# Two layout turns of a two-block network on one Trainium2 core: TensorE transposes replaced by VectorE block transposes and SBUF transfers

## What is computed

```python
h = rmsnorm(x, norm1_g);  proj = h @ w_in
uv, s5_in, qkv, gates = ...                      # columns of proj
y_a = u * (tril(W_s) @ rmsnorm(v) + b_s)         # u, v = halves of gelu(uv), per chunk of 128 tokens
y_b = s5_mixer(s5_in)                            # linear state space scan, gelu, a gate g @ w_glu
y_c = stick_breaking_attention(q, k, v)
merged = sum(sigmoid(gates) * (y_n @ w_branch[n]))
x = x + merged @ w_out;  x = x + relu(rmsnorm(x) @ w_mlp_in)**2 @ w_mlp_out;  x = rmsnorm(x)
```

## Time and profile before

| | |
|---|---|
| three timed runs | 2872.83 us median, 2872.74 to 2873.57 |
| the profiled execution | 2873.68 us, of which its span is 2872.0 |
| TensorE matmuls busy | 2855.1 us, 99% of the span |
| weight loads, VectorE, ScalarE busy | 2358.0, 1813.5, 1368.5 us |
| granted TensorE clock | 1.0 |
| DMA | 588.38 MB, 205 GB/s |

### The profile page before, as it was taken

One profiled execution on the slowest core, in us unless ns is written; L12 is line 12 of the kernel. 1 busy time (PEld: TensorE's weight loads), 2 busy tenths in 40 slices (PEclk: granted clock), 3 DMA queues, 4 the chain that ended last, 5 costly groups with the idle time before them and its releaser, 6 DMA issues.

```text
span 2872.0 us, 33479 instructions
## 1 busy us (share of the span) xinstructions
PE 2855.1 (99%) x13486; PEld 2358.0 (82%) x13486; DVE 1813.5 (63%) x1939; ACT 1368.5 (48%) x1534; POOL 2.0 (0%) x7
## 2 busy tenths in 40 slices
PE   9999999999999999999999999999999999999998
PEld 7888878888888888888888888888888888888887
DVE  7688854466765556555567678866675555556555
ACT  6644444564455444444446444454455444444444
POOL 0000000000000000000000000000000000000000
PEclk9999999999999999999999999999999999999999
DMA  9566656546867666665667656656667666666664
GB/s 317 153 201 198 205 163 196 169 156 199 256 220 216 211 203 214 203 209 194 202 218 225 208 182 198 201 195 204 204 216 234 221 204 193 212 202 215 203 209 165
DMA packets 347354, 588.38 MB, mean 205 GB/s; under 512 B 21056, under 2 KB 81088, under 8 KB 346560
## 3 DMA queue, kind: packets, MB, share of 16 engines
q1 hardware_dynamic: 346768, 585.93, 64.1%
q10 hardware_dynamic: 432, 0.32, 0.0%
HBM read 556.81 MB, written 2.10 MB: 195 GB/s over the span
## 4 chain that ended last, share of the span: by engine, by line
PE 95%; DVE 3%; ACT 1%; issue 1%; DMA 0%; SPq 0%; DVEq 0%; ACTq 0%
PE ACC L633 93%; DVE WL L1308 1%; PE TB L579 0%; ACT WH L883 0%; DMA RAW<-in_w_in_dram 0%; PE TB L693 0%; DVE HT L1707 0%; DVE CA L1829 0%; DVE WGC L1877 0%; PE TB L726 0%; PE TB L729 0%; PE TB L735 0%; DVE ZCb L1682 0%; PE TB L781 0%; PE TB L835 0%
## 5 line engine op out<-in xcount | busy, mean ns | idle before, releaser
L1308 DVE TENSOR_TENSOR WL<-RAW,WH 128x1024 fp32r<-128x1024 f32 (+1 forms) x1023 | 1229.9, 1217 | 832.9 <-ACT WH L883 828.7
L883 ACT ACTIVATE WH<-RAW 128x1024 fp32r<-128x1024 f32 (+1 forms) x1023 | 1064.2, 1054 | 1120.0 <-PE ACC L633 797.2
L633 PE MATMUL ACC<-WH,XTH 128*128 128x512 f32 (+1 forms) x1692 | 662.1, 391 | 5.0 <-DVE WL L1308 3.4
L633 PE MATMUL ACC<-WH,XTL 128*128 128x512 f32 (+1 forms) x1692 | 655.6, 387 | 0.0
L633 PE MATMUL ACC<-WL,XTH 128*128 128x512 f32 (+1 forms) x1692 | 655.3, 387 | 0.0
L633 PE MATMUL ACC<-WH,XBL 128*128 128x512 f32 x1024 | 398.4, 389 | 0.0
L633 PE MATMUL ACC<-WH,XBH 128*128 128x512 f32 x1024 | 398.4, 389 | 0.0
L633 PE MATMUL ACC<-WL,XBH 128*128 128x512 f32 x1024 | 398.3, 389 | 0.0
L633 PEld LDWEIGHTS ACC<-WH,XTH 128*128 128x128 f32 x1692 | 317.8, 188 | 74.1 <-DVE WL L1308 6.7
L633 PEld LDWEIGHTS ACC<-WH,XTL 128*128 128x128 f32 x1692 | 317.7, 188 | 65.7
L633 PEld LDWEIGHTS ACC<-WL,XTH 128*128 128x128 f32 x1692 | 318.0, 188 | 62.7
(11 more groups left out here) (274 smaller groups left out, 1611.9 us busy)
## 6 DMA issues: line engine op xcount, KB each, us to landing
RAW<-in_w_in_dram SPq DMA_DIRECT2D x255, 512.0 KB, 4.3
RAW<-in_w_mlp_in_dram SPq DMA_DIRECT2D x128, 512.0 KB, 4.2
RAW<-in_w_mlp_out_dram SPq DMA_DIRECT2D x128, 512.0 KB, 4.9
RAW<-in_w_up_dram SPq DMA_DIRECT2D x128, 512.0 KB, 4.1
RAW<-in_w_down_dram SPq DMA_DIRECT2D x128, 512.0 KB, 4.8
RAW<-in_w_gate_dram SPq DMA_DIRECT2D x96, 512.0 KB, 4.3
YT<-HT SPq DMA_DIRECT2D x208, 128.0 KB, 2.7
RAW<-in_w_branch_dram SPq DMA_DIRECT2D x48, 512.0 KB, 4.3
```

What stands on the lines that cost most here:

```text
L633: ins = e.matmul(ACC[:, 2 * (b % 2) + half, 0:n], p[:, k, xs], q[:, t, 0:n], start=(k == 0 and m == 0), stop=(k == nk - 1 and m == 2))
L883: e.activation(WH[u % NSPL][:, :, 0:n], RAW[u % NRAW][:, :, 0:n], ACT.Copy).then_inc(hi, 1)
L1308: e.tensor_tensor(l, r, h, ALU.subtract).then_inc(lo, 1)
```

## The change

Both turns leave TensorE. VectorE transposes blocks of 32 by 32 (`block_turn`), four transfers for each half of the channels place them, and ScalarE and VectorE read the result from SBUF.

For the input, the turns stand behind units 16 and 17 on VectorE, the transfers ahead of the loads of units 23 and 24 on SyncE, and ScalarE's copies (`ut`) behind unit 24 instead of 25. They are four copies to `UT` and then, after a wait for these, eight from `UT` to `UP`.

For the output, VectorE's turns stand behind units 43 and 51, the transfers ahead of the loads of units 50 and 58, and the copy to `YAH` and the subtraction to `YAL` behind 49 and 57.

```diff
+    XIT = [(pool[:, 2048 + 1024 * c:3072 + 1024 * c].rearrange("p (g h n) -> p g h n", g=4, h=2),
+            pool[:, 1024 * c:1024 * c + 1024].rearrange("p (h t n) -> p h t n", h=2, t=4)) for c in range(2)]
+    UGT = (X[:, 0, 0:1024].rearrange("p (g h n) -> p g h n", g=4, h=2), X[:, 0, 1024:2048].rearrange("p (h t n) -> p h t n", h=2, t=4))
...
-    banks("ut", 4, (0, 1, 2, 3))
-    banks("gm0", 4, (2, 3))
-    banks("gm1", 4, (2, 3))
+    banks("gm0", 2, (2, 3))
+    banks("gm1", 2, (2, 3))
...
-    at("ut", 25)
+    XIT_AT, UGT_AT = (16, 17), (43, 51)
+    for u in XIT_AT:
+        at("xin_turn", u)
+    at("ut", 24)
...
-    at("gm0", 41, 4)
-    at("gm1", 49, 4)
+    at("gm0", 41, 2)
+    at("gm1", 49, 2)
+    for u in UGT_AT:
+        at("ug_turn", u)
+        at("ug_split", u + 6)
...
+            for c, (t_, y) in enumerate(XIT):
+                if u == XIT_AT[c] + 7:
+                    e.wait_ge(xin_turned, c + 1)
+                    for t in range(4):
+                        e.dma_start(y[:, :, t, :], t_[32 * t:32 * t + 32, :, :, :]).then_inc(xin_moved[c], 16)
+            for c in range(2):
+                if u == UGT_AT[c] + 7:
+                    e.wait_ge(ug_turned, c + 1)
+                    if c:
+                        e.wait_ge(ug_lo, c)
+                    for t in range(4):
+                        e.dma_start(UGT[1][:, :, t, :], UGT[0][32 * t:32 * t + 32, :, :, :]).then_inc(ug_moved[c], 16)
...
-                emptied(e, f"gm{i // 2}", 2 + i % 2)
+                e.wait_ge(ug_lo, i // 2 + 1)
...
-        def ut():
-            evicted(e, "s5in", 0)
-            evicted(e, "s5in", 1)
-            e.wait_ge(ld["cst"], 16)
-            for k in range(4):
-                t, done = bank("ut", k)
-                transposes(t, lambda m, half: XIN[:, half, (2 * k + m) * P:(2 * k + m) * P + P]).then_inc(done, 1)
-            yield
...
+                e.wait_ge(up_done, 1)
...
-            for k in range(2):
-                if k == 0:
-                    emptied(e, f"gm{c}", 1)
-                t, done = bank(f"gm{c}", 2 + k)
-                transposes(t, lambda m, half: UG[c][:, half, (2 * k + m) * P:(2 * k + m) * P + P]).then_inc(done, 1)
-                yield
...
         def ut():
...
+            for c in range(2):
+                e.wait_ge(xin_moved[c], 64)
+                for h in range(2):
+                    ins = e.activation(UT[:, 4 * c:4 * c + 4, h * P:h * P + P].rearrange("p k (t i) -> p t k i", t=4),
+                                       XIT[c][1][:, h, :, :].rearrange("p t (k i) -> p t k i", k=4), ACT.Copy)
+            ins.then_inc(ut_done, 1)
+            e.wait_ge(ut_done, 1)
+            for q in range(8):
+                ins = e.activation(UP[:, q, :].rearrange("p (k i c) -> p k i c", k=2, i=8),
+                                   UT[:, q, :].rearrange("p (c i k) -> p k i c", i=8, k=2), ACT.Copy)
+            ins.then_inc(up_done, 1)
...
+        def ug_split():
+            for c in range(2):
+                e.wait_ge(ug_moved[c], 64)
+                e.activation(by_tokens(YAH[:, 4 * c:4 * c + 4, :]), UGT[1].rearrange("p h t (k i) -> p (h t) k i", k=4), ACT.Copy
+                             ).then_inc(ug_hi, 1)
                 yield
...
+        def block_turn(t_, src, done):
+            for half in range(2):
+                ins = e.transpose(t_[:, :, half, :].rearrange("p g (k i) -> p k g i", k=4),
+                                  src[:, half, :].rearrange("p (k j g) -> p k g j", k=4, g=4))
+            ins.then_inc(done, 1)
+
+        def xin_turn():
+            e.wait_ge(squared, SQUARED[R_X0])
+            for c in range(2):
+                evicted(e, "s5in", c)
+                block_turn(XIT[c][0], XIN[:, :, 512 * c:512 * c + 512], xin_turned)
+                yield
+
+        def ug_turn():
+            for i in range(4):
+                filled(e, ("bu", 3), i)
+            for c in range(2):
+                emptied(e, f"gm{c}", 1)
+                if c:
+                    e.wait_ge(ug_moved[0], 64)
+                block_turn(UGT[0], UG[c], ug_turned)
+                yield
+
+        def ug_split():
+            for c in range(2):
+                e.wait_ge(ug_hi, c + 1)
+                e.tensor_tensor(by_tokens(YAL[:, 4 * c:4 * c + 4, :]), UGT[1].rearrange("p h t (k i) -> p (h t) k i", k=4),
+                                by_tokens(YAH[:, 4 * c:4 * c + 4, :]), ALU.subtract).then_inc(ug_lo, 1)
                 yield
```

More of the change, by code:

```diff
@@ L163, in build @@
     moved = [sem(f"turned_moved{i}") for i in range(2)]
+    xin_turned, ut_done, up_done = sem("s5_input_turned"), sem("s5_input_placed"), sem("s5_input_ordered")
+    xin_moved = [sem(f"s5_input_moved{c}") for c in range(2)]
+    ug_turned, ug_hi, ug_lo = sem("gm_turned"), sem("gm_hi"), sem("gm_lo")
+    ug_moved = [sem(f"gm_moved{c}") for c in range(2)]
     za_sig, ua_prod, pads = sem("glu2_sigmoid"), sem("glu2_product"), sem("pads")
@@ L320, in build @@
     banks("lg", 3, (0, 1))
-    YA0 = {"gm0": 0, "gm1": 2, ("at_o", 0): 4, ("at_o", 1): 6}
+    YA0 = {("at_o", 0): 0, ("at_o", 1): 2}
     TURNS = []
@@ L682, in s5_bu @@
                 e.wait_ge(ld["s5b"], 64)
+                e.wait_ge(up_done, 1)
                 for k in range(4):
                     emptied(e, "ab", k)
-                    emptied(e, "ut", k)
             to = [bank(("bu", r), i) for i in range(4)]
@@ L849, in pool_groups @@
                 yield
-        tasks = {"ab": ab, "ut": ut, "k0": k0, "gm0": lambda: gm(0), "gm1": lambda: gm(1), "glu_gate": glu_gate, "at_t": at_turn,
+        tasks = {"ab": ab, "k0": k0, "gm0": lambda: gm(0), "gm1": lambda: gm(1), "glu_gate": glu_gate, "at_t": at_turn,
                  "ua": lambda: plain_turn("ua", ZA, lambda: e.wait_ge(ua_prod, 1)),
@@ L1259, in _ @@
                  ("ev", "qkv"): lambda: qkv_out(), ("ev", "glu"): glu_out,
-                 "gm0": lambda: gm_turn(0), "gm1": lambda: gm_turn(1), "at_t": at_turn, "yb": yb,
+                 "ug_split": ug_split, "at_t": at_turn, "yb": yb,
                  "split": split,
@@ L1580, in gm @@
                 yield
-            for k in range(2):
-                kk = 4 * c + 2 * k
-                low_part(YAL[:, kk:kk + 2, :], YAH[:, kk:kk + 2, :], ya_hi, YA0[f"gm{c}"] + k + 1, f"gm{c}", 2 + k)
+        def block_turn(t_, src, done):
[23 more added lines that the diff above has]
+                                by_tokens(YAH[:, 4 * c:4 * c + 4, :]), ALU.subtract).then_inc(ug_lo, 1)
                 yield
@@ L1645, in gate_out @@
                 if g == "ga" and c == 0:
-                    filled(e, "gm1", 2)
-                    filled(e, "gm1", 3)
+                    filled(e, "gm1", 1)
+                    e.wait_ge(ug_turned, 2)
                 if g == "gc" and c == 0:
@@ L1893, in _ @@
         tasks = {"x_split": x_split, "x_norm": x_norm, "s5_par": s5_par, "s5_mat": s5_mat, "s5_out": s5_out, "scan": s5_scan, "v_norm": v_norm,
-                 "gm0": lambda: gm(0), "gm1": lambda: gm(1), "gt": lambda: place("gt", UT, 8), ("ev", "glu"): glu_out,
+                 "gm0": lambda: gm(0), "gm1": lambda: gm(1), "xin_turn": xin_turn, "ug_turn": ug_turn, "ug_split": ug_split, "gt": lambda: place("gt", UT, 8), ("ev", "glu"): glu_out,
                  "glu_gate": glu_gate, "yb": lambda: place("yb", UT, 8),
```

## The result

| | before | changed |
|---|---|---|
| median of six runs each, same chip | 2873.44 us (2872.74 to 2874.60) | 2882.36 us (2881.11 to 2883.77) |
| profiled execution, its span | 2873.68, 2872.0 us | 2883.77, 2882.0 us |
| ratio of the times | | 1.003 (95% interval 1.0021 to 1.004) |

The change costs 8.9 us by the medians and 10.1 us by the two profiled executions. The forecast was 5.0 us; the measured time of 2882.36 us lies 1.4 us above the upper end of the range.

A forecast was written before the change was run, and what follows sets the result against it. TensorE was taken to bound the kernel, its matmuls busy for 99% of the span. VectorE's turns +3.96, ScalarE's copies +2.8 and the output -1.8 gave +5.0 us, forecast as 2878.0 us, range 2876.7 to 2880.0.

The forecast's parts named there:

- The bound and the two places: TensorE bounds the kernel; the places to look at are the `ab` transposes behind unit 22, and unit 26.
- VectorE's turns: Two pairs of input transposes behind units 16 and 17, ahead of line 1469: all 3.96 us lost, bounds 3.9 to 4.3.
- The transfers: Four issues on SyncE ahead of the weight loads of units 23 and 24: cost nil, up to 2.7 us without cover.
- The output's half: First mixer's output: TensorE's transposes leave the chain, gain 1.8 us, bounds 2.0 and 0.9 if VectorE is late twice.
- The source is SBUF, not PSUM ... I take 0.31.: ScalarE's `ut` copies: 0.31 us for each copy of 256 elements, from a line through copies of 512 and 1024.
- 4 x 0.53 + 8 x 0.31 + 0.15: Length of ScalarE's twelve `ut` copies behind unit 24, with 0.15 for the wait between groups: 4.75 us.
- the second term: ScalarE's copies one unit earlier make TensorE stand before unit 27: net loss 2.8 us, bounds 2.0 to 3.8.
- the chance of 0.10 for the clock: Rival, chance 0.10: pauses before units 26 and 27 bring 1.2 GHz for one or two units; 2880.7 to 2883.5 us.
- The 0.2 us added for VectorE's sequencer: Allowance for waits of some 0.1 us that VectorE's sequencer adds, taking 2877.8 to 2878.0 us.
- the transposes are a plain gain: Rival, chance 0.08: VectorE's turns and ScalarE's copies find room, TensorE loses 3.7 us of transposes; 2869.1 or 2870.8 us.
- Only VectorE's turns cost: Rival, chance 0.12: ScalarE gets to unit 27 in time, so the sum is 2.0 us; 2874.8 us.
- the wait for `UP`: TensorE's new wait before `s5_bu` behind unit 27: nil, as it ends at 87.65, covered by unit 27.

The follow-up runs named there:

- e7_fill38: The changed kernel with 38 matmuls, whose result nobody reads, put on TensorE into the pause before unit 27; 2880.02 us, ratio 1.0024 to the kernel before.
- e5_plain_order: The changed kernel with ScalarE's eight copies to `UP` reading `UT` in sequence, so tokens are not reordered; 2879.15 us, ratio 1.0018 to the kernel before.
- e1_ut25: The changed kernel with ScalarE's `ut` copies put back behind unit 25 instead of 24; 2875.90 us, ratio 1.0007 to the kernel before.
- e4_fill: The changed kernel with 20 matmuls, whose result nobody reads, put on TensorE into the pause before unit 27; 2881.50 us, ratio 1.0026 to the kernel before.

## Why the prediction was wrong

**What held.** The bound and the two places. VectorE's turns: +3.96 forecast, +3.90 measured. `ab` was to start at 76.5 and started at 76.35. The wait at `ab` had been 0.4 us; the waits of the changed kernel, 60 to 125 us (total, times, longest):

```profile
PEld ACC L658 <- DVE WL L1318: 9.4, 4, 4.8
...
PEld TB L691 <- DVE SS L1479: 2.0, 1, 2.0
```

The split was as told: a part near unit 20, which is 1.8 us, and most of the rest at `ab`. `ut` was to begin at 86.9 and began at 86.71. The transfers cost nothing in these places, as said. The Trainium skill's price of a VectorE transpose (page "VectorE: DVE Perf Modes", section "The three transpose paths") is 311 ns for 128 by 128 in bf16; the estimate from it was 5.0 for this term. The trace does not agree: in float32 four such pieces take 1.0 us, the pair of instructions as in the earlier trace rows (VectorE in time, changed kernel):

```profile
62.73 2.04 DVE L1594 STREAM_TRANSPOSE SS<-X 128x512 f32<-128x512 f32 x2
...
162.03 2.07 DVE L1594 STREAM_TRANSPOSE X<-GR 128x512 f32<-128x512 f32 x2
```

The output's half: -1.8 forecast, -1.93 measured.

**What failed first: "The source is SBUF, not PSUM ... I take 0.31."** The step "4 x 0.53 + 8 x 0.31 + 0.15" gave 4.75 us; it took 6.45, from 86.71 to 93.16. The first four were priced right. The eight took 0.53 each, because I drew a line through copies that read in sequence and looked at the number of elements alone; that the source expression in the diff, `"p (c i k) -> p k i c"`, steps over 16 elements did not enter. With the same stride out of PSUM it had cost nothing that one could see in the earlier trace rows. The 1.7 us too little are just what the second term came out too small: 2.8 forecast, 4.53 measured, beyond its bound of 3.8, which had taken 0.40 for a copy. The Trainium skill, page "SBUF — State Buffer", section "Door 1: The DMA port swizzle (why `[64,N]` ≈ `[32,N]`)", says that SBUF has lines of 16 bytes and that each access that crosses to a new line pays. By that rule steps of 64 bytes pay with each element, which agrees with 0.53 against 0.31 us for 256 of them; I had not looked there.

**What failed second: the chance of 0.10 for the clock.** The rival had the place (the pause before unit 27), the mechanism and nearly the price: one to two units at 2.73 us each, measured 2.58. That the pause brought it is shown by the filled pause. The Trainium skill, page "TensorE: Matmul & The Clock Gate", section "HAM oscillation", warns that idle gaps between bursts of matmuls bring the lower level; e7_fill38 agrees, as no stretch at 0.50 is left there once the gap is filled. That the rival's 2880.7 to 2883.5 us holds the measured time is in part luck: it has the copies at 2.8 us, and its upper end supposes two slow units where one came. I had weighed it with "the rows of before show no pause as long", which is no evidence against it: the sum itself had just made a pause of 2.9 us that no row of before could show. And it was not independent of the first error: the pause came out at 4.38 us and not 2.9. But the forecast's own pause of 2.9 us would in most executions have been enough, for 2.57 us of idleness already cost 1.7 in the profile of e5_plain_order. With that price, which I know only from this run, 3.96 + 2.8 + 1.7 - 1.8 is 6.7, or about 2880, so the clock should have had far more than 0.10.

**What nobody foresaw:** up to 1.0 us at `k0`, which goes with a late transfer of instructions. Without it the profiled execution would lie 9.1 above before.

So of the 5.1 us between forecast and profiled execution 1.7 are the copies, 2.6 the clock and 1.0 the stand at `k0`; the rest, -0.2, is the small differences of the other terms. The 0.2 us added for VectorE's sequencer to get from 2877.8 to 2878.0 showed nowhere: the term it belongs to came out at 3.90 us, under its 3.96. Of the rivals, "the transposes are a plain gain" fell as the rows had said. "Only VectorE's turns cost" did not come in the changed kernel; it is near to what e1_ut25 measures, 2875.9 against 2874.8, where 0.8 us are the wait for `UP` behind unit 27. In the forecast that wait was nil because `ut` stood one unit ahead; that is the one thing for which the early place was good, 0.8 us of cover for 7.1 us of loss.

## What to carry to other kernels

Before a task of several microseconds is put on an engine that also feeds the bound engine, look at what stands behind it in that engine's order: the same twelve copies cost 0.8 us behind unit 25 and 7.1 us behind unit 24, because the weights of one unit were made after them and not before. Price a copy by memory and by stride on each side, not only by its number of elements. And when a sum makes a pause of TensorE that was not there, count the lower clock after it as part of the price, not as a case apart: in the profiles here pauses of 2.1 to 4.4 us cost 1.7 to 2.6 us more each, though not in every execution.

## What the runs showed of the hardware

- A ScalarE copy of 128 by 256 elements in float32 took 0.26 us with 64-byte steps out of PSUM, 0.31 out of SBUF in sequence, 0.45 with writes scattered by 512 bytes and 0.53 with 64-byte steps on an SBUF source. I had not expected SBUF to be the dearer source, nor strided writes to cost.
- The clock's fall came, in the profiles, after pauses as short as 2.08 us of idleness (with one of 1.6 shortly before), lasted 3.41 or 6.83 us, and began up to 1.3 us after TensorE had started again: in e4_fill the unit began at 95.58 and the clock fell at 96.89. With 2.57 us idle it did not fall in three of ten executions.
- TensorE stood for 0.4 to 0.8 us in a row of 128 small matmuls in two profiles and not in others of nearly equal programs. The later a transfer of 16 KB of instructions landed (0.39 and 0.70 us after the row began), the more was lost (0.68 and 1.00 us).
